# A hybrid transformer layer on one core: weight-sum transfers moved and sent one at a time, and another order of the last blocks

## The reference, cut to what matters

```python
def hybrid_mixer(h, ...):
    proj = h @ w_in                                    # 1024 -> 7 * 1024
    b_a, c_a, v_a, x_b, g_b, u_a, u_b = jnp.split(proj, SPLITS, axis=-1)
    y_a = b_a * causal_dwconv(c_a * v_a, conv_a_w, conv_a_b)
    x_b = causal_dwconv(x_b, conv_b_w, conv_b_b)
    y_b = rg_lru(x_b, ...) * jax.nn.gelu(g_b)          # gates: two block-diagonal products, then a scan
    m = jax.nn.sigmoid(u_a) * (y_a @ w_a_out) + jax.nn.sigmoid(u_b) * (y_b @ w_b_out)
    return m @ w_o

mod = (silu(c) @ w_mod + b_mod); sh_m, sc_m, gt_m, sh_f, sc_f, gt_f = split(mod)
h = rms_norm(x, g_pre_mix) * (1 + sc_m) + sh_m
x = x + gt_m * rms_norm(hybrid_mixer(h, ...), g_post_mix)
h = rms_norm(x, g_pre_mlp) * (1 + sc_f) + sh_f
y = square(relu(h @ w_mlp_up)) @ w_mlp_down            # 1024 -> 4096 -> 1024
x = x + gt_f * rms_norm(y, g_post_mlp)
```

## Time and profile before

| | us |
|---|---|
| three runs | 824.96, 829.25, 834.65 |
| median | 829.25 |
| the profiled execution | 823.69 |
| its span, first to last instruction | 822.0 |
| PE busy | 798.3 (97%) |
| DVE busy | 564.9 (69%) |
| ACT busy | 477.4 (58%) |
| POOL busy | 82.1 (10%) |
| mean granted PE clock | 0.993 of full speed |

### The profile page before, as it was taken

The page is one execution under the profiler, slowest core; times in us unless marked ns, Lnnn a source line. Parts: engine busy times, 40 slices in busy tenths (PEclk is TensorE's granted clock), DMA queues, the critical chain, the costliest instruction groups (busy, mean ns, idle before and its releaser), DMA issues.

```text
span 822.0 us, 12177 instructions
## 1 busy us (share of the span) xinstructions
PE 798.3 (97%) x4196; PEld 687.4 (84%) x4196; DVE 564.9 (69%) x714; ACT 477.4 (58%) x682; POOL 82.1 (10%) x94
## 2 busy tenths in 40 slices
PE   8999999999998999999799999999999999999996
PEld 7887788888886877877688889999999988888884
DVE  4776676665565556555677568877777598887777
ACT  6557777766643444434424466766666676555663
POOL 1640000002222122212211000000000000000000
PEclk9999999999999999999999999999999999999999
DMA  9961433329999999999997703233333396655502
GB/s 311 347 170 33 116 109 108 108 77 255 186 272 304 322 307 315 303 305 309 308 305 221 231 1 103 59 109 109 108 105 108 116 373 194 204 188 186 191 1 102
DMA packets 150949, 155.73 MB, mean 189 GB/s; under 512 B 5868, under 2 KB 118660, under 8 KB 150660
## 3 DMA queue, kind: packets, MB, share of 16 engines
q1 hardware_dynamic: 139300, 121.71, 47.2%
q0 software_dynamic: 11552, 33.57, 17.0%
q10 hardware_dynamic: 64, 0.02, 0.0%
HBM read 153.18 MB, written 35.65 MB: 230 GB/s over the span
## 4 chain that ended last, share of the span: by engine, by line
PE 64%; DMA 22%; DVE 6%; ACT 3%; issue 2%; SPq 1%; DVEq 0%; ACTq 0%; POOL 0%
PE ps L446 21%; PE ps L447 21%; PE ps L448 21%; DMA raw<-in_w_in_dram 9%; DMA w_dn_sums<-in_w_mlp_down_dram 4%; DMA raw<-in_w_b_out_dram 3%; DMA modraw<-in_w_mod_dram 3%; DVE modb L1388 2%; DMA raw<-in_w_a_out_dram 2%; ACT w_hi L757 1%; DMA mod_raw<-in_w_mod_dram 1%; DVE w_lo L1198 1%; DMA graw<-in_w_gate_i_dram 1%; DMA erows<-in_b_mod_dram 1%; SPq L620 0%
## 5 line engine op out<-in xcount | busy, mean ns | idle before, releaser
L446 PE MATMUL ps<-ht_hi,w_hi 128*128 128x512 f32 x448 | 175.6, 392 | 0.0
L447 PE MATMUL ps<-ht_lo,w_hi 128*128 128x512 f32 x448 | 174.8, 390 | 0.0
L448 PE MATMUL ps<-ht_hi,w_lo 128*128 128x512 f32 x448 | 174.6, 390 | 0.0
L1198 DVE TENSOR_TENSOR w_lo<-raw,w_hi 128x1024 fp32r<-128x1024 f32 x68 | 82.9, 1224 | 75.3 <-ACT w_hi L757 74.4
L757 ACT ACTIVATE w_hi<-raw 128x1024 fp32r<-128x1024 f32 x68 | 71.2, 1053 | 107.8 <-DMA raw<-in_w_in_dram 63.4
L446 PEld LDWEIGHTS ps<-ht_hi,w_hi 128*128 128x128 f32 x448 | 84.4, 188 | 18.8 <-issue 1.0
L448 PEld LDWEIGHTS ps<-ht_hi,w_lo 128*128 128x128 f32 x448 | 84.4, 188 | 17.8
L447 PEld LDWEIGHTS ps<-ht_lo,w_hi 128*128 128x128 f32 x448 | 84.4, 188 | 17.3
L446 PE MATMUL ps<-w_hi,hd_hi 128*128 128x512 f32 x224 | 87.4, 390 | 1.7 <-DVE w_lo L1571 1.7
L448 PE MATMUL ps<-w_hi,hd_lo 128*128 128x512 f32 x224 | 87.2, 389 | 0.0
L447 PE MATMUL ps<-w_lo,hd_hi 128*128 128x512 f32 x224 | 87.2, 389 | 0.0
(11 more groups left out here) (255 smaller groups left out, 1706.9 us busy)
## 6 DMA issues: line engine op xcount, KB each, us to landing
raw<-in_w_in_dram SPq DMA_DIRECT2D x48, 512.0 KB, 5.8
w_dn_sums<-in_w_mlp_down_dram POOLq DMA_DIRECT2D x48, 512.0 KB, 8.3
modraw<-in_w_mod_dram SPq DMA_DIRECT2D x32, 512.0 KB, 8.7
up_raw<-in_w_mlp_up_dram SPq DMA_DIRECT2D x56, 256.0 KB, 3.6
raw_y<-w_dn_sums SPq DMA_DIRECT2D x24, 512.0 KB, 4.2
mod_raw<-in_w_mod_dram SPq DMA_DIRECT2D x32, 256.0 KB, 7.6
w_dn_sums<-w_dn_sums POOLq DMA_DIRECT2D x16, 512.0 KB, 6.3
raw<-in_w_mlp_down_dram SPq DMA_DIRECT2D x12, 512.0 KB, 4.8
```

The costliest lines, as they stand in the source:

```text
L446: nc.tensor.matmul(dst, l_hi, r_hi, start=first, stop=False, skip_group_check=chained)
L447: nc.tensor.matmul(dst, l_hi, r_lo, start=False, stop=False, skip_group_check=chained)
L448: return nc.tensor.matmul(dst, l_lo, r_hi, start=False, stop=last, skip_group_check=chained)
L1198: V.tensor_tensor(w_lo[:, slot, :], raw[:, slot, :], f(w_hi[:, slot, :]), ALU.subtract).then_inc(w_lo_ready, 1)
```

## The change

The transfers that build the weight sums go one after the other, each waiting for the one before (one semaphore, `sums_in`). The first 11 pieces are sent in the mix stage, one per two units, from unit 10 on; the clearing of `modb` and the load of `b_mod` stand between them. None is sent between then and unit 64 (`U_BOUT`); the other 21 follow from there. At the end PE takes each group with `tb` = 0 and then `tb` = 1, and some of the row work of ACT and DVE comes one group later.

```diff
+        def sums_count(n):
+            return 32 * n
...
                 if p in SUMS and c == 0:
-                    for l in range(2):
-                        sp_eng.wait_ge(pool_in[l], lane_count(l, (SUMS.index(p) + 1) * CHUNKS // 2, 1))
+                    sp_eng.wait_ge(sums_in, sums_count(CHUNKS * (SUMS.index(p) + 1)))
                 load_chunk(i)
...
-            for i in range(4):
-                pool.wait_ge(unit_done, 4 * NB // 2 + 4 * i)
-                nc.gpsimd.memset(modb[:, i * D:(i + 1) * D], 0.0).then_inc(zeromb_ready, 1)
-            pool.wait_ge(zeromb_ready, 4)
-            pool.dma_start(modb[0:1, :], b_mod[0:1, 2 * D:6 * D]).then_inc(pool_in0, 16)
...   (the two-lane loop shown above is removed)
+            def sum_piece(n):
+                dst, start, more = pieces[n]
+                wait(pool, sums_in, sums_count(n))
+                pool.dma_start(dst, start).then_inc(sums_in, 16)
+                pool.wait_ge(sums_in, sums_count(n) + 16)
+                pool.dma_start(dst, more, accum_op=ALU.add).then_inc(sums_in, 16)
+
+            EARLY_SUMS, EARLY_UNIT, ZERO_UNIT = 11, N_FIRST + 4, 4 * NB // 2
+            for n in range(EARLY_SUMS):
+                u = EARLY_UNIT + 2 * n
+                i = (u - ZERO_UNIT) // 4
+                pool.wait_ge(unit_done, u)
+                if u == ZERO_UNIT + 4 * i and 0 <= i < 4:
+                    nc.gpsimd.memset(modb[:, i * D:(i + 1) * D], 0.0).then_inc(zeromb_ready, 1)
+                    if i == 3:
+                        pool.wait_ge(zeromb_ready, 4)
+                        pool.dma_start(modb[0:1, :], b_mod[0:1, 2 * D:6 * D]).then_inc(pool_in0, 16)
+                sum_piece(n)
+            pool.wait_ge(unit_done, U_BOUT)
+            for n in range(EARLY_SUMS, len(pieces)):
+                sum_piece(n)
...   ACT
-                if a == D_END + 1:
+                if a == D_END + 2:
                     (z_second for t = 2 and 3)
-                if a == D_END + 2:
+                if a == D_END + 3:
                     (z_first for t = 0 and 1)
...   DVE
-                if D_END + 1 <= a < D_END + 3:
-                    t = a - D_END + 1
+                if a >= D_END + 2:
+                    t = a - D_END
                     (z_gain of row block t, both halves)
...   PE: groups 26 and 27
-            for tb in range(2):
-                for a in range(D_END + DGROUPS - 2, D_END + DGROUPS):
+            for a in range(DGROUPS * PRODUCTS):
...
+                for tb in range(2):
```

More of the change, by code:

```diff
@@ L263, in hybrid_layer_kernel @@
         pool_in0 = sem("pool_in0")
-        pool_in1 = sem("pool_in1")
+        sums_in = sem("sums_in")
         gbc_in = sem("gbc_in")
@@ L395, in hybrid_layer_kernel @@
                    rows_in9, rows_in10, rows_in11, rows_in12, rows_in13]
-        pool_in = [pool_in0, pool_in1]
         raw0_in = [raw0_in0, raw0_in1, raw0_in2, raw0_in3, raw0_in4, raw0_in5, raw0_in6, raw0_in7]
@@ L486, in chunk_rows @@
             return w_sums[SUMS.index(p), c] if p in SUMS else w_dn_part(*DOWN_PART[p], c)
-        def lane_count(l, n, step):
-            return 16 * (2 * n - 1 + step + (l == 0))
+        def sums_count(n):
+            return 32 * n
         def sum_pieces():
@@ L725, in _ @@
             nc.gpsimd.memset(cvp[:, 0:KA - 1], 0.0).then_inc(const_ready, 1)
-            for i in range(4):
-                pool.wait_ge(unit_done, 4 * NB // 2 + 4 * i)
-                nc.gpsimd.memset(modb[:, i * D:(i + 1) * D], 0.0).then_inc(zeromb_ready, 1)
-            pool.wait_ge(zeromb_ready, 4)
-            pool.dma_start(modb[0:1, :], b_mod[0:1, 2 * D:6 * D]).then_inc(pool_in0, 16)
-            pieces = list(sum_pieces())
[L735 to L743, removed]
+            pieces = list(sum_pieces())
+            def sum_piece(n):
[18 more added lines that the diff above has]
+                sum_piece(n)
         @block.scalar
@@ L1961, in _ @@
                           D_S4: (d_copied, copied_count(D_S1, 0)), D_A22: (d_summed, summed_count(D_S3, 0))}
-            def down_block(a, tb):
+            pe.wait_ge(relu_ready, NCONV)
+            for a in range(DGROUPS * PRODUCTS):
                 p, g = divmod(a, DGROUPS)
[L1965 to L1977, removed]
                 if a == DGROUPS * D_A12:
@@ L1985, in _ @@
                 for tb in range(2):
-                    down_block(a, tb)
-            for tb in range(2):
-                for a in range(D_END + DGROUPS - 2, D_END + DGROUPS):
+                    if g == 0 and p in DOWN_AFTER:
+                        semaphore, count = DOWN_AFTER[p]
+                        pe.wait_ge(semaphore, count + tb)
                     if tb == 0:
-                        pe.wait_ge(hd_lo_ready, a + 1)
-                    down_block(a, tb)
+                        mm = down(a, tb, range(GROUP))
+                        if g == DGROUPS - 1:
+                            mm.then_inc(prod_done, 1)
+                    else:
+                        down(a, tb, range(GROUP // 2)).then_inc(unit_done, 1)
+                        down(a, tb, range(GROUP // 2, GROUP)).then_inc(unit_done, 1)
 _INS = ['x', 'c', 'w_mod', 'b_mod', 'g_pre_mix', 'g_post_mix', 'w_in', 'conv_a_w', 'conv_a_b',
```

## The result

The changed kernel takes 806.55 us (median of 4 runs, 805.61 to 810.15); the kernel before, with one more run beside it, 827.85 us (824.96 to 834.65). The ratio is 0.9736 (95% interval 0.9677 to 0.9794). Beside more runs of the kernel before, taken with the experiments (11 to 17 at a time, medians 824.7 to 825.9), the changed kernel's ratio is 0.9787: part of the first one is the high median of four runs. The profiled execution is the slowest of the four: 810.15 us, with a span of 808.5. The lines of the kernel have moved a little: the three-matmul helper is now L445 to L447, the gate stage's L1822 is L1827, the sums' two transfers are L731 (copy) and L733 (add).

What follows compares the result with a forecast made beforehand. PE bounds the kernel, in the gate stage now and then transfers not needed before 670 us. 823.7 - 11.6 - 2.75 + 1.0 - 1.1 = 809.2, plus 0.8: 810 us, range 806 to 817.

Steps and rivals of the forecast that it cites:

- rival A: The forecast itself: gate stage becomes PE's, small change elsewhere; 810 us (807 to 813), chance 0.66.
- Term 1: Gate stage without sums: loads land in 4 to 6 us; gain 11.6 us of waits plus 2.75 of half clock.
- the correction added at the end: 0.8 us added to the sum of 809.2, because the profiled run was 5.6 us under the runs' median.
- term 4: End of the down product: group 27's stall of 1.7 us goes, DVE 0.6 late; net gain 1.1 us (0 to 1.7).
- Term 2: The 11 early pieces in the mix stage: 11.6 us a piece, cost 0, at the bound 4 us.
- Term 3: The 21 late pieces from unit 64: cost 1.0 us at w_o's k = 7 load (0 to 4.4), last ending at 632 us.
- The floor: Least that the matmul stream allows: 807.6 us; 806 with the runs' difference of 1.3 us on their fast side.
- B: Cost returns after unit 64: k = 7 comes 3 us late with half clock, further waits follow; 815 us, chance 0.15.
- C: Half the gate stage's waits stay, since SP, ACT and DVE wait for each other in a round; 816.5 us, chance 0.10.
- D: Sums come too late for the down product, PE stalls above 16.9 us a piece; slower than before, chance 0.03.
- E: Early pieces fall behind and fill the gate stage after all, or other loads do; 820 to 826 us, chance 0.06.

Runs made afterwards that it cites:

- single-lane kernel: Changed kernel's one transfer at a time, but all 32 pieces sent without a pause from about 193 us through the gate stage: 805.87 us, ratio 0.9776.
- paused kernel: Changed kernel, with POOL waiting after three late pieces until the eighth w_o block is split: 805.57 us, ratio 0.9776.
- moving the two gains back: Kernel with POOL's pause at w_o, plus DVE's gains for rows 128 to 255 back in groups 25 and 26: 805.43 us, ratio 0.9766.
- the one without sums: Changed kernel with no weight-sum transfers; SP loads a plain quarter of the down weights in place of each sum: 805.79 us.
- the trace of 829.9 us: Third trace of the kernel before, unedited, run again for its scatter: profiled execution 829.9 us, median of its 8 runs 826.77 us.

## Why the prediction was right or wrong

**What it said and what came.** It said 810 us and the median is 806.55, 3.5 lower, and 0.45 under the band of 807 to 813 that rival A, the forecast, gave itself. The direction and the order of the terms held, and so did the mechanism as far as sums in flight made the gate stage's loads late. The step that failed is the size of the first term, "all five waits, 11.6 us, and the half clock", 2.75: it was put at 14.35 us and measured 16.5. That is 2.1 of the 3.5 us; 0.8 is the correction added at the end, and 0.5 the size of term 4.

**Term 1, the gate stage: mechanism right, size wrong.** All five L1822 waits went and the clock stayed at 1.00, as forecast; loads land in 4.9 us ("4 to 6"). But the term was taken as 11.6 + 2.75 = 14.35 us and measured 16.5 (from -0.27 to 16.19). By the table: the five waits gave 3.85 + 1.17 + 1.08 + 1.94 + 4.35 = 12.4 us and `yb_lo`'s, which the sum left out, 0.4. Each is 0.16 us more than its idle time, because a matmul of this size is shown 0.39 us long while the next starts 0.227 after it. The two half clocks gave 1.5 and 1.6 us, so 3.2 (5.11 - 3.59 + 16.19 - 14.55) and not 2.75: the stretches of 2.5 and 3.0 us that they were read from leave out their edges. The last 0.5 us came in small steps between. What was wrong in the step is this: idle time read off the waits was taken as time lost, when the time from start to start is what counts.

**The cause was put on placement, and it is pacing.** "Without queue 0 the loads there need 52.9% of the engines" is the reason that the step gave. That figure was a share held while PE was being stopped, and not the need: with queue 0 gone, queue 1 held 66.1% and moved 33.0 MB from 215 to 390 us, where it had held 52.9% and moved 28.9. The single-lane kernel keeps queue 0 in the gate stage at 33.6%, has loads of 7.4 us and loses nothing. So a load may take 7.4 us there, but not 11.9; the whole gain of the gate stage is had by taking the second lane away, and the placement on top of it (the early pieces, the pause in the gate stage) adds nothing that could be measured: 805.87 against 806.6 on another chip.

**Term 2, the early pieces: right.** Cost 0. A piece took 13.1 us (82.4 to 213.6 for ten) and not 11.6, so that the add of the eleventh was sent only at 217.64, where its end was forecast for 212, with no effect. `b_mod` was issued at 195.11 (194 forecast).

**Term 3, the late pieces: right in the median, with some luck.** 1.0 us was the forecast; changed kernel less paused kernel is 806.6 - 805.57 = 1.0. Single traces have 0, 0.8 and 4.4, and the landing of 5.1 us that it was worked out from was 4.3, 4.9 and 7.3 in them. In the profiled run it was 2.77 of wait and 1.6 of half clock, 4.4, which is the upper bound that the step gave. The last piece ended near 659 instead of 632, with 12.8 us a piece for 11.6: well inside the 15.9 that it needed.

**Term 4, the end: 1.1 forecast, 1.6 measured** in the matched traces (2.1 less 0.5). PE gained 2.1 us and not 1.7: the stall was again more than its idle time. The lateness of DVE is 0.5 us for the 0.6 forecast, and moving the two gains back takes it away.

**The correction and the floor: wrong.** With 16.5 and 1.6 in place of 14.35 and 1.1 the sum is 823.7 - 16.5 + 1.0 - 1.6 = 806.6 us, the median. The 0.8 us added for the higher median of before had no ground. Most of the 5.6 us between that median and the profiled execution came from having three runs; over 11 to 17 runs the median is 824.7 to 825.9, 1 to 2 us above. What makes single runs longer are longer half clocks in the gate stage, which go with its waits, and the w_o wait (6.2 us between two traces), of which the changed kernel keeps 0.6 to 2.6 us. The runs of before spread over 9 us, those of the changed kernel over 1.5 in six of its runs (and once 810.15). The floor of 807.6 was built on the same 14.35; it is 805.6 to 805.8, as the paused kernel and the one without sums show.

**The rivals.** B (the cost comes back after unit 64, 815): its first part did happen in one execution, with its 4.4 us, and the further waits did not. The Trainium skill, DMA: Bandwidth & Descriptors, section "Issuing engines are not separate DMA queues", says that transfers interleave on the same 16 engines whoever issues them. This case's traces agree: POOL's pieces raised the mix stage's loads from 3.8 to 6.3 us, which SP issues, and PE waited for none of them. C (half of the waits stay): no L1827 wait, the round of SP, ACT and DVE was not what held PE. D (the sums too late): 12.8 us a piece against 16.9. The 32 issues of L733 took 1025 to 1071 ns, about as in the earlier trace rows, with DVE busy 70% of the span, so these traces show no hold-up of POOL's issues. E (the sums fill the gate stage after all, 820 to 826): it didn't come, and its price was wrong as well: the single-lane kernel is just that case, and takes 805.87.

## What to carry to other kernels

Before moving a background transfer out of a stage, try with one of its lanes taken away: in this kernel a stream with a deadline far off ran beside a stage whose loads held 61% of the engines, at no cost, once only one of its transfers flew at a time. When a wait is turned into a gain, count from the start of the matmul before it to the start of the one behind it, and the slow matmuls that follow, by their starts; the idle time in a row is the lower end. And a kernel that scatters by 9 us is telling of waits that come and go: one trace of it shows one draw, so a second one is worth reading before the terms are sized.

## What the runs showed of the hardware

- Landing time of a 512 KB load, at the median, against the DMA share of its stretch: 3.8 us at 0.37, 4.9 at 0.70, 6.3 at 0.78, 7.4 at 0.94, 11.9 at 1.07. In the last step the bytes moved rise by a sixth, from 253 to 296 GB/s, and the landing by 60%.
- A piece (copy of 512 KB within the chip's memory, then an accumulating transfer of as much, one behind the other) takes 12.8 to 13.1 us beside other loads, and the two land in 4.5 and 6.9 us at the median.
- Behind PE waits of 2.6, 3.7 and 4.2 us the granted clock was about 0.5 (1.2 GHz) for the next seven to nine matmuls. After waits of 0.9 to 1.8 us it stayed at 1.00 (2.4 GHz) in the trace of before; in the trace of 829.9 us one of 2.0 us was followed by 0.50 (373.5 to 376.3 us) and one of 1.8 us by 0.57 (465 to 469 us). With the same idle time in total, how much of this followed made a good part of the difference between two executions of one kernel.
